# Scaling the attention probabilities of a hybrid decoder step on GpSimd instead of VectorE

## What is computed

```python
def masked_softmax(s, mask):
    s = jnp.where(mask, s.astype(jnp.float32), NEG)
    m = jnp.max(s, axis=-1, keepdims=True)
    p = jnp.where(mask, jnp.exp(s - m), 0.0)
    return p / jnp.maximum(jnp.sum(p, axis=-1, keepdims=True), 1e-30)

# per query block of 128 tokens, 8 heads in 2 groups of 4, head dim 64, ALiBi slopes
o_c = compressed_branch(...)   # 64 compressed keys
o_s = selected_branch(...)     # with 1024 tokens, all 16 blocks of 64 are selected: causal attention
o_w = window_branch(...)       # the last 512 keys
g = sigmoid(gl)
o = g[..., 0:1] * o_c + g[..., 1:2] * o_s + g[..., 2:3] * o_w
```

## Time and profile before

| what | value |
|---|---|
| median of three runs | 2548.51 us (2546.48 to 2560.22) |
| profiled execution, its own time | 2567.4 us |
| span of its instructions | 2565.5 us |
| mean granted TensorE clock | 0.938 of full |
| TensorE matmul / VectorE / ScalarE / GpSimd busy | 92% / 43% / 28% / 4% of the span |
| prompt attention in that span | about 217 to 552 us |

### The profile page before, as it was taken

The page is one execution under the profiler, slowest core; times in us unless marked ns, Lnnn a source line. Parts: engine busy times, 40 slices in busy tenths (PEclk is TensorE's granted clock), DMA queues, the critical chain, the costliest instruction groups (busy, mean ns, idle before and its releaser), DMA issues.

```text
span 2565.5 us, 31435 instructions
## 1 busy us (share of the span) xinstructions
PE 2355.1 (92%) x13082; PEld 1858.5 (72%) x13082; DVE 1111.2 (43%) x2059; ACT 730.1 (28%) x1354; POOL 94.3 (4%) x94
## 2 busy tenths in 40 slices
PE   7987899979679999999669999997999999999995
PEld 7966776669336667777448888545988988988883
DVE  2144777666320006565541111354444344454446
ACT  3214666545320113434221101122211111211216
POOL 0020000001100000000000000000000000000003
PEclk9985998889979999999769999998999999999998
DMA  4422000026550111110131111311111111111101
GB/s 143 80 65 80 2 2 1 1 71 202 191 173 9 33 41 26 29 32 1 34 99 50 42 33 42 115 34 51 57 42 50 42 42 50 42 42 50 33 17 66
DMA packets 148327, 141.89 MB, mean 55 GB/s; under 512 B 32985, under 2 KB 133937, under 8 KB 143834
## 3 DMA queue, kind: packets, MB, share of 16 engines
q1 hardware_dynamic: 143322, 106.06, 14.2%
q0 software_dynamic: 4864, 33.82, 3.9%
HBM read 130.63 MB, written 13.42 MB: 56 GB/s over the span
## 4 chain that ended last, share of the span: by engine, by line
PE 67%; ACT 2%; DVE 2%; DMA 2%; issue 1%; POOLq 0%; POOL 0%; DVEq 0%; SPq 0%; ACTq 0%
PE PS L628 36%; PE PS L659 13%; PE PS L1074 5%; PE PS L1048 4%; DMA arena<-in_cache_sel_kv,arena 2%; PE PS L920 1%; PE PS L988 1%; PE PS L999 1%; PE PS L1004 1%; PE PS L1013 1%; PE PS L979 1%; PE PS L897 1%; ACT L1376 0%; ACT arena L1378 0%; PE PS L1018 0%
## 5 line engine op out<-in xcount | busy, mean ns | idle before, releaser
L628 PE MATMUL PS<-w_down_high,hidden 128*128 128x512 f32 (+1 forms) x1152 | 364.8, 395 | 11.8 <-DVE arena L1888 7.4
L628 PE MATMUL PS<-x_low,w_high_mlp 128*128 128x344 f32 x1152 | 369.2, 320 | 0.0
L659 PE MATMUL PS<-xT,wring 128*128 128x344 f32 x1152 | 339.0, 456 | 1.5 <-DVEq L1646 1.5
L659 PEld LDWEIGHTS PS<-xT,wring 128*128 128x128 f32 x1152 | 219.7, 191 | 115.3 <-issue 2.3
L1888 DVE TENSOR_TENSOR arena<-arena,PS 128x512 f32<-128x512 f32 (+1 forms) x288 | 196.6, 685 | 148.0 <-PE PS L628 148.0
L628 PEld LDWEIGHTS PS<-w_down_high,hidden 128*128 128x128 f32 (+1 forms) x1152 | 204.3, 177 | 74.6 <-DVE arena L1888 9.7
L628 PE MATMUL PS<-x_high,w_high_mlp 128*128 128x344 f32 x768 | 246.4, 321 | 5.9 <-DVE w_low L641 5.9
L628 PE MATMUL PS<-x_high,w_low 128*128 128x344 f32 x768 | 246.1, 320 | 0.0
L628 PE MATMUL PS<-w_down_low,hidden 128*128 128x512 f32 (+1 forms) x576 | 226.8, 394 | 0.0
L628 PEld LDWEIGHTS PS<-x_low,w_high_mlp 128*128 128x128 f32 x1152 | 218.1, 189 | 2.9
L628 PEld LDWEIGHTS PS<-x_high,w_high_mlp 128*128 128x128 f32 x768 | 144.9, 189 | 8.0 <-issue 6.0
(11 more groups left out here) (317 smaller groups left out, 3678.1 us busy)
## 6 DMA issues: line engine op xcount, KB each, us to landing
wring<-in_w_in SPq DMA_DIRECT2D x100, 256.0 KB, 3.3
wring<-in_w_up SPq DMA_DIRECT2D x64, 256.0 KB, 3.3
arena<-in_w_down SPq DMA_DIRECT2D x16, 1024.0 KB, 4.9
arena<-in_x_prompt SPq DMA_DIRECT2D x16, 512.0 KB, 5.5
out<-arena SPq DMA_DIRECT2D x9, 512.0 KB
arena<-in_cache_win_kv SPq DMA_DIRECT2D x8, 512.0 KB, 3.4
arena<-in_w_out SPq DMA_DIRECT2D x2, 2048.0 KB, 9.3
out<-in_cache_win_kv SPq DMA_DIRECT2D x1, 4088.0 KB
```

What stands on the lines that cost most here:

```text
L628: mm = pe.matmul(out, w, x, start=(k == 0 and i == 0), stop=(k == tiles - 1 and i == 2))
L659: mm = pe.matmul(unit_out(x, m, cn), wring[:, n % WR, k, 0:m], xT[:, k, c0:c0 + cn], start=(k == 0), stop=(k == KD - 1))
```

## The change

The two multiplications of `scale` leave VectorE's queue and stand in GpSimd's, in a loop over all 128 jobs behind the position rows. VectorE's reciprocal no longer waits for its own completion; it counts a new semaphore `rc_dve` for which GpSimd waits. TensorE's `turn` waits for GpSimd's `p_pool` in place of `p_dve`, and in window jobs also for the new `pc_pool`, counted by the multiplication of the compressed columns. The order of VectorE's queue is otherwise what it was: the reciprocal of job j+1 stands behind the maxima of job j+2. The two casts of L1918 move in GpSimd's queue from ahead of the loop to behind the scaling of job 8, with waits for their own completion.

```diff
@@ -760,7 +761,9 @@
                 if gi == 0:
-                    pe.wait_ge(p_dve, j + 1)
+                    pe.wait_ge(p_pool, j + 1)
+                    if wc:
+                        pe.wait_ge(pc_pool, j // 4 * 2 + j % 2 + 1)
                     if j >= 1:
                         pe.wait_ge(t_act, j)
@@ -1483,13 +1486,7 @@
                 w = 2 if wc else 1
                 if wc and i == 0:
                     steps(dve.tensor_scalar(sm[:, 5:6], sm[:, 5:6], 1e-30, None, ALU.max))
-                steps(dve.reciprocal(sm[:, 8:8 + w], sm[:, 4:4 + w]))
-                gt = gates[:, i, 3 * h:3 * h + 3]
-                if wc:
-                    mark(dve.tensor_scalar(pr[:, j % 2, 640:704], pr[:, j % 2, 640:704], sm[:, 9:10], gt[:, 0:1], ALU.mult, ALU.mult))
-                n = P * (i + 1) if not wc else P * min(i + 1, 5)
-                dve.tensor_scalar(pr[:, j % 2, 0:n], pr[:, j % 2, 0:n], sm[:, 8:9], gt[:, 1 + wc:2 + wc], ALU.mult, ALU.mult
-                                  ).then_inc(p_dve, 1)
+                dve.reciprocal(sm[:, 8:8 + w], sm[:, 4:4 + w]).then_inc(rc_dve, 1)
@@ -1911,11 +1908,27 @@
             pool.tensor_copy(kc2[64:65, :, :], posrow[:, SEQ:].rearrange("a (g n) -> a g n", g=2)).then_inc(ka_pool, 1)
-            pool.wait_ge(ka_act, 4)
-            pool.wait_ge(ka_dve, 8)
-            pool.wait_ge(ka_pool, 2)
-            for br in range(2):
-                pool.tensor_copy(k2[br][1][64:65, :], k2[br][0][64:65, :].bitcast(F32)).then_inc(ka_pool, 1)
+
+            for j in range(NJ):
+                h, i, wc = job(j)
+                sm = small[:, 16 * (j % 4):16 * (j % 4) + 16]
+                gt = gates[:, i, 3 * h:3 * h + 3]
+                pool.wait_ge(rc_dve, j + 1)
+                if j == 0:
+                    pool.wait_ge(ka_pool, 3)
+                if wc:
+                    pool.tensor_scalar(pr[:, j % 2, 640:704], pr[:, j % 2, 640:704], sm[:, 9:10], gt[:, 0:1], ALU.mult, ALU.mult
+                                       ).then_inc(pc_pool, 1)
+                n = P * (i + 1) if not wc else P * min(i + 1, 5)
+                pool.tensor_scalar(pr[:, j % 2, 0:n], pr[:, j % 2, 0:n], sm[:, 8:9], gt[:, 1 + wc:2 + wc], ALU.mult, ALU.mult
+                                   ).then_inc(p_pool, 1)
+                if j == 8:
+                    pool.wait_ge(ka_act, 4)
+                    pool.wait_ge(ka_dve, 8)
+                    pool.wait_ge(p_pool, 9)
+                    for br in range(2):
+                        pool.tensor_copy(k2[br][1][64:65, :], k2[br][0][64:65, :].bitcast(F32)).then_inc(ka_pool, 1)
+                    pool.wait_ge(ka_pool, 5)
```

More of the change, by code:

```diff
@@ L258, in hybrid_step @@
         ka_act, ka_dve, ka_pool, pos_in = sem("k_high_staged"), sem("k_low_staged"), sem("positions_staged"), sem("positions_loaded")
-        q_s, ss_ps, e_act, m_dve, p_dve, q_row = (sem("q_staged"), sem("scores_ready"), sem("exp_done"), sem("max_done"),
+        q_s, ss_ps, e_act, m_dve, p_pool, q_row = (sem("q_staged"), sem("scores_ready"), sem("exp_done"), sem("max_done"),
                                       sem("probs_scaled"), sem("slope_row_set"))
-        dch = sem("dve_steps")
+        dch, rc_dve = sem("dve_steps"), sem("row_sums_inverted")
+        pc_pool = sem("cmp_probs_scaled")
         t_ps, t_act, t_dve, pv_ps, o_act = (sem("probs_turned"), sem("probs_copied_act"), sem("probs_copied_dve"),
```

## The result

The changed kernel took 2578.94 us (median of 4 runs, 2572.44 to 2582.84), the kernel before 2550.02 us in its four; the ratio is 1.0101, with a 95% interval of 1.0072 to 1.013. A second comparison on another chip gave 1.0093 (1.0068 to 1.0118). So the change costs about 1%, 24 to 29 us.

What follows compares the result with a forecast made beforehand. The prediction took the latency of a chain through VectorE's even-job scaling to bound the prompt attention; 19 us of dearer scalings plus about 1 us of waits, put on the 2548.5 us median, gave 2569 us, range 2550 to 2602.

Steps and rivals of the forecast that it cites:

- The round, and the 52 tight even jobs: Prompt attention: scores, odd maximum, even scaling, turn, pv; 52 of 64 even jobs turn within 0.06 us of scaling.
- Nothing is won by emptying VectorE: Prompt attention: removing 192 multiplications from VectorE's queue gains nothing, since odd maxima wait for TensorE; costed at nothing.
- The price of a scaling on GpSimd: Each GpSimd scaling in prompt attention estimated at 0.15 us plus 1.3 us per 1000 columns; terms together 19 us.
- Low bound, a copy's price: GpSimd scaling costs at least a copy, 0.15 + 0.89 us per 1000 columns; the sum then is 6 us.
- Hand-over to GpSimd: Reciprocal's end to GpSimd's scaling start takes 0.08 us, 0.04 more than before, in each tight job.
- One more satisfied wait, about 1 us: TensorE's turns: one extra, already satisfied wait in 64 turns costs about 1 us.
- GpSimd 128x640 at about 1.0 us: Sign in the profile after: a GpSimd scaling group of 640 columns takes about 1.0 us (0.72 in rival 1).
- Rival 1: GpSimd scales at 0.89 to 1.05 us per 1000 columns: +6 to +11 us, 2554 to 2560; chance 0.28.
- Rival 2: GpSimd scaling at two-input price or worse, above 1.6 per 1000: +28 to +72 us, likeliest 2589; chance 0.22.
- Rival 3: Prompt attention's mean TensorE clock falls from 0.86 to 0.75 after more stalls: +18 us on top, 2587; chance 0.06.
- Rival 4: Faster: emptier VectorE brings odd maxima forward or half-clock stretches shorten, up to -15 us; chance 0.04.
- Contention, up to 4 us: VectorE's two-input staging beside GpSimd's odd scalings, six times at 0.65 us each, 4 us at most.

Runs made afterwards that it cites:

- runs split by parity: Changed kernel with half the scalings back on VectorE: even jobs on VectorE, odd on GpSimd, ratio 1.001; mirror, odd on VectorE, even on GpSimd, 1.0113.
- exchange for even jobs: Even job's scaling moved ahead of the next job's maxima in the kernel before: ratio 0.9894; its reciprocal moved likewise in the changed kernel: 0.9907.
- second pair: Kernel before and changed kernel, both unchanged, profiled again on one chip: spans 2546.5 and 2568.5 us, ratio 1.0093.

## Why the prediction held

The forecast was 2569 us, 2550 to 2602; 2579 was measured, a loss of 24 to 29 us where 20 were forecast. The mechanism is shown by the runs split by parity, and again by the exchange for even jobs. That the number came so near is in part luck, as the price of a scaling shows.

- *The round, and the 52 tight even jobs*: right. The tight jobs stayed tight, the odd ones loose. Of the 12 loose even jobs, taken at nothing, most turned tight in the first profile after (59 even jobs tight in place of 52); the small selected ones cost 0.9 us. One exception among the odd: the two casts behind job 8, costed at nothing, made TensorE wait 0.58 us for odd job 9.
- *Nothing is won by emptying VectorE*: right as far as the profiles show; its waits for TensorE grew from 82 to 139 us (68 to 138 in the second pair).
- *The price of a scaling on GpSimd*, taken as 0.15 + 1.3 per 1000 columns: this is the term that was mis-sized, in both parts. Measured, 0.34 + 0.83. At 640 columns the two agree (0.98 and 0.88), so the 15 large windows came out near (6.2 forecast, 7.0 measured); at 1024 it was too dear, so the selected jobs were overestimated (10.2 and 7.3); at 64 columns too cheap (0.23 and 0.40), which with the fixed part made the small windows twice what was forecast (2.7 and 5.9). The sum of 19 us against 21 comes from errors that cancel.
- *Low bound, a copy's price*: the slope came out a little below it (0.83 and 0.89), the fixed part well above. "A scaling reads and writes as much as a copy" was right of the columns and silent on the instruction.
- *Hand-over to GpSimd*, 0.08 us: 0.11 measured (284.13 to 284.24).
- *One more satisfied wait, about 1 us*: no row stood behind this term, and none bears it out. From the end of the scaling to the turn, tight window jobs, which have the added wait, take 0.054 us after the change and 0.056 before, as selected jobs without it do.
- *GpSimd 128x640 at about 1.0 us, transposes waiting about 48 us in about 50 turns, VectorE at 150 us*: 0.88 us, 54.4 us in 58, 164 us. VectorE's 150 was the sum of the single times; its records overlap their neighbours by some 0.08 us (223.62 + 0.31 ends behind 223.85 in the earlier trace rows), so that 90 us of instructions were only 77 us of busy time.
- *The stage some 20 us longer*: 26.8 in the second pair of profiles. Waits account for 22.0 and TensorE's longer busy time for 3.2.
- *Rival 1, a copy's price*: the slope said yes, the fixed part no; it ended beyond its point of 12.7 us. *Rival 2* fell: no two-input price. *Rival 3, the clock*: 0.92 and 0.91 in the second pair, and about 2 us of the loss over all runs; in the first pair the clock favoured the changed kernel, so that its two spans showed a sixth of the loss. The rival's sum was too small by half: a mean that falls from 0.86 to 0.75 over 335 us means 74 us more at half clock, not 37, and up to 37 us lost, not 18. *Rival 4* fell.
- *Contention, up to 4 us*: there, but small. The two-input staging (L1427, now L1430), from which the 4 us were worked out, never met a scaling: its instructions take 0.68 to 0.69 us, before and after. One-input staging did: one-row instructions six times, for 0.17 us on VectorE or 0.22 us on GpSimd each, and a cast in job 3 once, for 0.49 us on GpSimd (0.89 in place of 0.40), 1.7 us in all and all in odd jobs. The Trainium skill ("SBUF — State Buffer", Who interferes with whom) has an exclusive lock on the shared ports, under which the engine that comes second blocks fully. The 0.78 us in place of 0.56 agree that the second one waits; the 42 ns beside VectorE's 64 columns show that it need not wait for as long as the first one's record lasts.
- The Trainium skill ("GPSIMD Engine Reference", Engine selection) advises VectorE for elementwise work, and calls one-input work on GpSimd roughly line rate. Here the same one-input scaling takes 1.3 to 1.5 times as long on GpSimd (451 and 344 ns at 128 columns, 1198 and 812 at 1024), so the trace bears out the first half and the second only roughly.

## What to carry to other kernels

Before work is moved to an idle engine, find the round of instructions that the bounding engine waits for and ask whether the work lies on it: the same multiplications cost nothing measurable in odd jobs and the whole loss in even ones. On GpSimd count instructions as well as columns; here one of 64 columns took 0.40 us. And where an engine's order puts a long instruction between an input that is ready and a result that is awaited, exchanging the two was worth 27 us in the kernel before, while the same exchange where the input was not ready cost some 60. Before two profiles are compared, look at their clocks and at where each lies among the runs of its kernel.

## What had not been expected of the hardware

- A scaling on GpSimd has about a copy's slope (0.83 us per 1000 columns), though it multiplies twice, but starts from 0.34 us, where copies and casts of other shapes give 0.15 to 0.18.
- VectorE and GpSimd block each other in single scalings, and how long depends on the columns: 42 ns of GpSimd's time for 64 columns on VectorE, 0.22 us for one row of 512.
- The granted clock made 14 us of difference in one stage between two executions of one kernel with the same instructions (0.86 and 0.92), TensorE's busy time being 16.7 us longer, which is why one pair of profiles showed a sixth of the loss that the medians showed.
